# Paged sample attention: keys turned on VectorE in 32x32 blocks instead of on TensorE, scores by 32x32 tiles, and the past bias laid out to match

## What is computed

```python
past_k  = cache_fox_k[page_table].reshape(db, past_len, H_F, D_F)      # db 8, past_len 4096, H_F 8, D_F 64
past_v  = cache_fox_v[page_table].reshape(db, past_len, H_F, D_F)
past_lf = cache_fox_logf[page_table].reshape(db, past_len, H_F)
c_all = cumsum(concat([past_lf, logf], axis=1), axis=1)
s = einsum('bqhd,bkhd->bhqk', q, concat(past_k, fk)) * D_F ** -0.5
s = s + c_all[query] - c_all[key]                                       # the bias; masked where key > query
p = softmax(s, axis=-1)
o = einsum('bhqk,bkhd->bqhd', p, concat(past_v, fv))                    # then @ w_fox_o, times a sigmoid gate
```

## Time and profile before

| | |
|---|---|
| median of 3 runs | 3672.9 us (3669.8 to 3675.2) |
| the profiled execution | 3673.46 us |
| its span | 3671.6 us |
| granted TensorE clock, mean | 0.949 |
| TensorE busy over the span | 3314.7 us (90%) |
| sample bias phase | 1720 to 1768 us |
| sample attention phase | 2091 to 2616 us |

### The profile page before, as it was taken

How to read it: one execution, slowest core, us unless ns; L and a number is a source line. 1 busy time by engine, 2 the same in 40 slices (tenths; PEclk the granted TensorE clock), 3 DMA queues, 4 the chain that set the end, 5 groups by cost and what they waited for, 6 DMA issues and landing times. The chain is left out here.

```text
span 3671.6 us, 56105 instructions
## 1 busy us (share of the span) xinstructions
PE 3314.7 (90%) x21121; PEld 2999.5 (82%) x21121; DVE 888.4 (24%) x1581; ACT 625.5 (17%) x1163; POOL 794.6 (22%) x696
## 2 busy tenths in 40 slices
PE   5999999997988898786799899999796999999996
PEld 5999999996887798554688666666686999999995
DVE  2111111114206211555101022222314111111114
ACT  3000000002101100344000144434203000000003
POOL 0232222323120131022111111111021223233220
PEclk8999999998997899899899999999798999999998
DMA  5111111111110112210211299999311111111111
GB/s 141 35 51 40 42 49 34 49 49 29 29 44 22 41 40 67 91 48 17 52 43 43 60 297 307 300 305 303 121 29 29 34 46 50 33 51 43 37 37 55
DMA packets 328667, 293.12 MB, mean 80 GB/s; under 512 B 33640, under 2 KB 249064, under 8 KB 328048
## 3 DMA queue, kind: packets, MB, share of 16 engines
q1 hardware_dynamic: 317136, 275.93, 24.3%
q0 software_dynamic: 11424, 15.76, 1.6%
HBM read 279.34 MB, written 12.26 MB: 79 GB/s over the span
## 5 line engine op out<-in xcount | busy, mean ns | idle before, releaser
L207 PE MATMUL f_acc<-x_hi,w_hi_last 128*128 128x364 f32 x1056 | 233.5, 329 | 27.5 <-SPq L489 27.5
L165 POOL CAST w_hi_first<-w_raw_first 128x1024 fp32r<-128x1024 f32 (+1 forms) x96 | 82.9, 863 | 738.4 <-issue 301.3
L207 PE MATMUL f_acc<-x_hi,w_hi_first 128*128 128x364 f32 x1056 | 233.5, 329 | 6.9 <-SPq L489 6.9
L207 PE MATMUL f_acc<-x_lo,w_hi_last 128*128 128x364 f32 x1056 | 234.0, 330 | 0.0
L207 PE MATMUL f_acc<-x_hi,w_lo_last 128*128 128x364 f32 x1056 | 234.0, 330 | 0.0
L207 PE MATMUL f_acc<-x_hi,w_lo_first 128*128 128x364 f32 x1056 | 233.9, 330 | 0.0
L207 PE MATMUL f_acc<-x_lo,w_hi_first 128*128 128x364 f32 x1056 | 233.7, 329 | 0.0
L207 PEld LDWEIGHTS f_acc<-x_hi,w_hi_last 128*128 128x128 f32 x1056 | 184.0, 189 | 28.0 <-issue 28.0
L165 POOL CAST w_hi_last<-w_raw_last 128x1024 fp32r<-128x1024 f32 (+2 forms) x92 | 73.5, 799 | 614.2 <-PE f_acc L207 610.2
L596 DVE SCALAR_TENSOR_TENSOR br<-f_acc,br 128x1092 f32 x88 | 114.1, 1296 | 368.8 <-PE f_acc L207 368.8
L207 PEld LDWEIGHTS f_acc<-x_hi,w_hi_first 128*128 128x128 f32 x1056 | 184.0, 189 | 7.1 <-issue 7.1
(11 more groups left out here) (399 smaller groups left out, 6321.8 us busy)
## 6 DMA issues: line engine op xcount, KB each, us to landing
br<-cache_fox_k SPq DMA_DIRECT2D x256, 256.0 KB, 5.6
br<-cache_fox_v SPq DMA_DIRECT2D x256, 256.0 KB, 6.5
w_raw_first<-w_ffn_gate SPq DMA_DIRECT2D x22, 512.0 KB, 3.8
w_raw_first<-w_ffn_up SPq DMA_DIRECT2D x22, 512.0 KB, 3.8
w_raw_last<-w_ffn_gate SPq DMA_DIRECT2D x22, 512.0 KB, 3.8
w_raw_last<-w_ffn_up SPq DMA_DIRECT2D x22, 512.0 KB, 3.8
w_raw_first<-w_ffn_down SPq DMA_DIRECT2D x40, 256.0 KB, 2.9
w_raw_last<-w_ffn_down SPq DMA_DIRECT2D x40, 256.0 KB, 2.8
```

Source lines behind the costliest of these rows:

```text
L165: self.nc.gpsimd.tensor_copy(hi, raw).then_inc(self.high[s], 1)
L207: mm = self.nc.tensor.matmul(out[:, b, 0:width], w[s][:, k, :], x[:, k, b * width:(b + 1) * width], start=(k == 0 and first), stop=(k == k ...
```

## The change

The work and its result stay what they were. Its parts:

1. **Page table.** One contiguous DMA in place of the two with a stride. The pages come in their natural order.
2. **Bias phase.** The sums are made 32 rows at a time, four of them in one PSUM tile by column group (rows 0 to 31, 32 to 63, and so on), and for every fourth page by itself. That makes 64 pairs of matmuls of 32 rows by 128 columns, 128 matmuls in place of 32, written so that the 8 of one column group follow one another. Their operands are first rearranged: 4 copies on ScalarE (`d_own`), 4 on VectorE (`d_behind`). `d_qz` is no longer made here.
3. **Turning the keys.** VectorE turns a quad by 2 instructions of 128x1024 that transpose every 32x32 block in place, into one of 2 tiles `d_kt`. The 16 transposes of a quad on TensorE and the 4 copies on ScalarE are gone. SP waits for `k_turned` once per half of a chunk instead of once per key page.
4. **Scores.** 64 matmuls per quad, with 32 rows of keys' dimensions, 32 rows of queries and 128 columns each: 4 row groups of the array write 4 PSUM banks, 4 column groups are 4 pairs of heads, and 4 matmuls add up in each place. The queries lie in `d_q_rep`, which ScalarE fills by 16 small copies per sequence (and 2 for the new tokens' `d_qz`).
5. **Behind the scores.** All heads' pages have their own column group, so a step has 512 columns for VectorE's minimum and ScalarE's exponentials (before: 256), 4 turns of probabilities (before: 2), 16 products of 128 columns (before: 8 of 256), and `d_acc` of 128 columns (before: 256). The copy to `d_pt` moves from VectorE to ScalarE. `d_stp`, `d_ptp` and `d_ov` have one buffer instead of two, so that `scores(k)` waits for the minimum of step k - 1. `swap`, `comb` and the combining at a sequence's end are gone.
6. **Fillers.** The gate and the `w_fox_o` product take the prompt in 3 blocks of up to 364 columns in place of 2 of 512 and a rest of 64.
7. **Ring.** The bias is loaded into `mem_kt` and `mem_v`, in 128 DMAs of 64 KB where there were 64 of 128 KB.

The core of the diff:

```diff
-                for e in range(2):
-                    half = g.pages[:].rearrange("o (b n e) -> o b n e", b=NSEQ, e=2)[:, :, :, e]
-                    sp.dma_start(half, io["page_table"][:, e * (NPG // 2):(e + 1) * (NPG // 2)].unsqueeze(0),
-                                 allow_slow_non_contiguous=True).then_inc(consts, 16)
+                sp.dma_start(g.pages[:], io["page_table"].rearrange("b n -> (b n)").unsqueeze(0)).then_inc(consts, 16)
...
                 pe.wait_ge(copied, 2)
-                pe.wait_ge(steps, 6)
+                pe.wait_ge(own_ok, QUAD)
+                pe.wait_ge(behind_ok, QUAD)
                 for c in range(2 * NSEQ):
                     if c == NSEQ:
                         pe.wait_ge(read, 1)
                     b, x = divmod(c, 2)
-                    own = lft[:, b, x * HG:(x + 1) * HG, :].rearrange("p g h -> p (g h)")
-                    behind = tot[1][:, b, x * HG + 1:(x + 1) * HG + 1, :].rearrange("p g h -> p (g h)")
-                    nc.tensor.matmul(sums[:, c % NSEQ, :], own, after[:], start=True, stop=False)
-                    mm = nc.tensor.matmul(sums[:, c % NSEQ, :], behind, g.ones[:], start=False, stop=True)
+                    group, pages = slice(ROWS * (c % 4), ROWS * (c % 4 + 1)), slice(x * QUAD, (x + 1) * QUAD)
+                    for n in range(QUAD):
+                        at = by_token[group, c // 4 % 2, n]
+                        nc.tensor.matmul(at, own[:, b, n, pages, :].rearrange("p u h -> p (u h)"), after[:],
+                                         start=True, stop=False, skip_group_check=True)
+                        mm = nc.tensor.matmul(at, behind[:, b, n, pages, :].rearrange("p u h -> p (u h)"), g.ones[:],
+                                              start=False, stop=True, skip_group_check=True)
...
+                for n in range(QUAD):
+                    nc.scalar.copy(own[:, :, n], lft[:, :, n:NPG:QUAD]).then_inc(own_ok, 1)
...
+                for n in range(QUAD):
+                    nc.vector.tensor_copy(behind[:, :, n], tot[1][:, :, n + 1:NPG + 1:QUAD]).then_inc(behind_ok, 1)
...
-                sp.dma_start(swap[:], io["swap"]).then_inc(const, 16)
-                sp.dma_start(comb[:], io["comb"]).then_inc(const, 16)
...
                 with sp.Fori(0, CHUNKS - 1) as c:
                     ahead, now = pages(c + 1), pages(c)
                     for half in range(2):
+                        sp.wait_ge(k_turned, c * 4 + (2 * half + 2))
                         for s in range(half * QUAD, (half + 1) * QUAD):
-                            sp.wait_ge(k_turned, c * CH + (s + 1))
-                            sp.dma_start(k_in[:, s, :], keys[ahead[s]].rearrange("t h d -> t (h d)")).then_inc(k_ok[s], 16)
-                        sp.wait_ge(valued, c * 8 + (4 * half + 4))
+                            load_key(s, ahead[s])
+                        sp.wait_ge(valued, c * 2 + (half + 1))
...
+                    out = stp_pages.rearrange("p n (f t) -> p n f t", f=QUAD)
+                    for s in range(2):
+                        for h in range(2):
+                            for x in range(4):
+                                rows = slice(ROWS * x, ROWS * (x + 1))
+                                for c in range(PAIRS):
+                                    block = 4 * c + 2 * s + h
+                                    q = q_rep[e][rows, block * QW - s * LSEQ:block * QW - s * LSEQ + ROWS]
+                                    mm = nc.tensor.matmul(out[ROWS * c:ROWS * (c + 1), x], q,
+                                                          kt[u % 2][rows, :, block * ROWS:(block + 1) * ROWS],
+                                                          start=(s == 0 and h == 0), stop=(s == 1 and h == 1),
+                                                          skip_group_check=True)
+                    mm.then_inc(scored, 1)
...
+                    for y in range(QUAD if v else 1):
+                        if v:
+                            n = u * QUAD + y
+                            pe.wait_ge(v_ok[n % CH], 16 * (n // CH + 1))
+                        for c in range(PAIRS):
+                            values = v_in[:, n % CH, c * P:(c + 1) * P] if v else g.v_s[0:TS, c * P:(c + 1) * P]
+                            mm = nc.tensor.matmul(ov[ROWS * c:ROWS * (c + 1), :],
+                                                  pt[0:P if v else TS, y, ROWS * c:ROWS * (c + 1)], values,
+                                                  start=(y == 0), stop=(y == QUAD - 1 or not v), skip_group_check=True)
+                    mm.then_inc(valued if v else new_valued, 1)
...
                 for k in range(STEPS_ALL + 4):
-                    u = quad_after(k)
-                    if u is not None:
-                        turn(u, 0)
-                        turn(u, 1)
+                    if k < STEPS_ALL:
+                        scores(k)
                     if 0 < k <= STEPS_ALL:
                         turn_probs(k - 1)
+                    fill(k)
                     if k >= PIECES + 1 and (k - 1) % PIECES == 0:
-                        swap_stats((k - 1) // PIECES - 1)
-                    if k >= PIECES + 2 and (k - 2) % PIECES == 0:
-                        turn_out((k - 2) // PIECES - 1)
-                    fill(k)
-                    if u is not None:
-                        turn(u, 2)
-                        turn(u, 3)
-                    if k < STEPS_ALL:
-                        scores(k)
+                        turn_out((k - 1) // PIECES - 1)
                     if 0 < k <= STEPS_ALL:
                         products(k - 1)
...
+                    nc.scalar.activation(out, least, ACT.Exp, bias=nm[e][:, v:v + 1], scale=-1.0,
                                          accum_out=lp[e][:, v:v + 1]).then_inc(exped, 1)
...
+                    nc.scalar.copy(pt[0:rows, 0:n], ptp[0:rows, 0:n]).then_inc(pt_ok, 1)
...
+                def turn(u):
+                    for s in range(u % 2 * QUAD, (u % 2 + 1) * QUAD):
+                        dve.wait_ge(k_ok[s], 16 * (u // 2 + 1))
+                    if u >= 2:
+                        dve.wait_ge(scored, step_of(u - 2) + 1)
+                    for y in range(2):
+                        nc.vector.transpose(kt[u % 2][:, 2 * y:2 * y + 2, :], k_in[:, u % 2, 2 * y:2 * y + 2, :])\
+                            .then_inc(k_turned, 1)
...
                 for k in range(STEPS_ALL + 4):
-                    if 0 < k <= STEPS_ALL:
-                        place(k - 1)
-                    if k >= PIECES + 1 and (k - 1) % PIECES == 0:
-                        finish((k - 1) // PIECES - 1)
-                    if k >= PIECES + 2 and (k - 2) % PIECES == 0:
-                        output((k - 2) // PIECES - 1)
-                    add_mix(k)
```

More of the change, by code:

```diff
@@ L2146, in phase_sample_bias @@
         after, upto = g.sb(ctx, "d_after", [P, P]), g.sb(ctx, "d_upto", [TS, TS])
-        mask, lfx = g.sb(ctx, "d_mask", [P, NSEQ, TS]), g.sb(ctx, "d_lfx", [TS, 2, 2, 4, LSEQ])
-        out = g.sb(ctx, "d_out", [P, 2 * NSEQ, P])
+        mask, lfx = g.sb(ctx, "d_mask", [P, NSEQ, TS]), g.sb(ctx, "d_lfx", [TS, PAIRS, ROWS])
+        own, behind = (g.sb(ctx, f"d_{x}", [P, NSEQ, QUAD, NPG // QUAD, H_F]) for x in ("own", "behind"))
+        out = g.sb(ctx, "d_out", [P, NSEQ // 2, QUAD * P])
         t = [g.ps(ctx, f"d_t{j}", [P, H_F, P]) for j in range(2)]
-        sums = g.ps(ctx, "d_sums", [P, NSEQ, P])
+        sums = g.ps(ctx, "d_sums", [P, 2, QUAD * P])
         cn = g.ps(ctx, "d_cn", [P, TS])
@@ L2498, in turn_probs @@
                     else:
-                        half, m = divmod(b * (PIECES - 1) + v - 1, QUAD)
-                        for x in range(2):
-                            mm = nc.tensor.transpose(ptp[:, k % 2, x, :], ring[half % 2][:, m, x, :], g.ident[:])
+                        for y in range(QUAD):
+                            mm = nc.tensor.transpose(ptp[:, y, :], probs[:, y, :], g.ident[:])
                     mm.then_inc(pturned, 1)
@@ L2505, in scores @@
                     b, v = divmod(k, PIECES)
[L2506 to L2519 removed]
+                    e, u = b % 2, b * (PIECES - 1) + v - 1
@@ new lines, in scores @@
+                    if k > 0:
+                        pe.wait_ge(topped, k)
+                    if k >= PIECES + 2 and v == 2:
+                        pe.wait_ge(out_ok, b)
+                    if v == 0:
+                        pe.wait_ge(q_ok, 18 * (b + 1))
+                        for c in range(PAIRS):
+                            mm = nc.tensor.matmul(stp[ROWS * c:ROWS * (c + 1), 0, 0:TS], qz[e][:, c, :], g.k_s[:, c, :],
+                                                  start=True, stop=True)
+                        mm.then_inc(scored, 1)
+                        return
@@ L2560, in gate_part @@
+                    nc.tensor.transpose(ot, on[:], g.ident[:]).then_inc(ot_ok, 1)
+                def gate_part(j, x, ks):
+                    if ks[0] == 0 and 4 * j + x > 0:
```

(11 more changed lines are left out.)

407 lines of the change are left out of this document (180 added, 227 removed).

## The result

| | before | after |
|---|---|---|
| median | 3674.1 us (4 runs, 3669.8 to 3675.7) | 3747.6 us (4 runs, 3743.7 to 3756.8) |
| profiled span | 3671.6 us | 3747.4 us |
| ratio | | 1.0206 (95%: 1.0184 to 1.0227) |

The change costs 74 us, twice the 37 that were forecast, and 5.6 us beyond the end of the range. In the two spans the 75.8 us divide as follows, by the starts of SP's first and last issues in each phase: load phase -3.8 us (the bias phase's first issue comes at 1716.88 instead of 1720.66), bias phase +17.3, loop of the sample phase to its last value pages +66, tail and the rest -4.

The account below looks back on a forecast made before the run. It took SP's queue as the bound, with instruction fetches lengthening issues they meet. Terms -2 + 22 - 1 - 6 + 20 + 3 + 1 = +37 on 3673.5 us gave 3710 us; range 3670 to 3742.

Parts of the forecast that it names:

- load phase: Page table loading: one contiguous issue replaces two strided ones of 1.53 us in all; -2 us (0 to -3).
- bias phase: Serial sums before the sample phase: four VectorE copies and 128 records per half instead of 32; +22 us (+7 to +26).
- tail: Last steps after the last page: a little longer in matmuls; +1 us.
- start of the sample phase: Head of SP's queue: one table load of 0.35 us and its twin leave; -1 us.
- SP's register instructions: SP's loop: eight register instructions in front of key issues leave, part returning as a wait; -6 us (0 to -12).
- instruction packets that meet SP's issues: SP's loop: about 60 more instruction fetches, lengthening issues by 0.34 us each on average; +20 us (0 to +63).
- SP's waits in the loop: Sample phase: late value pages' places at sequence ends, with single buffers, make SP wait; +3 us (0 to +20).
- TensorE per step: Sample phase: scores of 0.9 us, a step of 4.2 to 4.8 us against SP's 7.7 per quad; term 0.
- The start of records decides: Rival, scores: TensorE begins at most one record per 62 ns, deciding above 30 ns; +256 us, 3966; 8% with anything worse.
- VectorE, or the single buffers, late: Rival, sample phase: transposes of 2.6 us and waits between engines push a quad past 7.7 us; +20, 3730 us; 8%.
- The overlap in the bias phase: Rival, bias phase: column groups run beside each other, making the phase's term +7; 3695 us; 15%.

Follow-up runs that it names:

- before_numbers_once: The kernel before, with SP's loop written out so that each page number is loaded into a register once instead of twice: 3632.9 us, ratio 0.9884.
- the control: The kernel before, with 4 matmuls of 128 columns on one column group added ahead of each quad's scores, which overwrite them: 3688.3 us, ratio 1.0044.
- VectorE's order: The changed kernel, turning the next quad's keys before this step's minimum: 3748.4 us; together with 32 score matmuls of 256 columns per quad: 3706.1 us.
- bias_by_columns: The changed kernel with the bias phase's 128 matmuls reordered, so the column group changes at each matmul instead of after 8: 3734.6 us, ratio 1.0175.
- before_more_instructions: The kernel before, with 56 matmuls of 4 columns added ahead of each quad's scores, which overwrite them: 3789.5 us, ratio 1.0315.

## Why the prediction was wrong

Right were the bound of the kernel before, which before_numbers_once confirmed, and the sign. Its terms:

| step | forecast | measured |
|---|---|---|
| load phase | -2 | -3.8 |
| bias phase | +22 | +17.3 |
| start of the sample phase | -1 | about 0 |
| SP's register instructions | -6 | -4 (ALU instructions 9.3 to 3.1 us, others 2 us more) |
| instruction packets that meet SP's issues | +20 | +15 (overrun 24.5 to 39.8 us) |
| SP's waits in the loop | +3 | +58 |
| tail | +1 | -3 to -4, with what lies behind it |

Seven terms, six of them within 5 us, read one by one from the traces (they add up to 79, not 76). The +15 stands against 55 more packets in the loop (34 before, 89 after; some 60 were forecast).

**The step that failed is "TensorE per step"**, with its sentence that TensorE has over 2.9 us to spare and its term is 0 up to 3.8 us of scores, and with it the +3 for waits: they came to 58 us more. Two things were wrong in it.

It counted the array's time, and got that too small. It has 4.2 to 4.8 us a step where TensorE is busy 7.1 us a quad, so that 0.6 us of SP's 7.7 were to spare and not 2.9. 128 score records take 1.64 us at the full clock, not 0.9. The pieces of the gate and of the `w_fox_o` product came to 3.1 us a quad, not 2.0 to 2.6. They have 364 columns in place of 512, but there are three of them in place of two and a small rest: 192 records of 364 columns for each kind of gate matmul, where 128 of 512 and 64 of 64 stood, which is as many columns. And 72 steps, not 64, fall on the 64 quads. The clock was granted less besides. The earlier trace rows had the check: 465.64 / 510 x 7.73 = 7.1 us busy a quad before, of which the turns that leave are 1.94. A busy TensorE is not yet late: before_numbers_once ran at 7.07 us a quad with TensorE busy 98%, and the control shows 0.86 us more per quad costing 16 us.

What the step left out is that the records have to be brought. The prediction had the packets, and their number nearly right, but looked at them only as something that SP's issues run into. The engine that consumes them stood in no term, although and the earlier trace rows gave the quotient: one packet per 232 to 250 records, and a quad of the change has some 360 records, where it had 130. Stops of up to 3.6 us followed, 69.6 us in all.

How much of the 58 us is theirs is only in part known. Without the stops the kernel is 29 us faster and SP's waits for keys are 41 us in place of 61; the shorter burst of scores has a share in the 29 that was not taken apart. VectorE's order gives some 13 us more, and about 23 us of waits stay open.

The rivals did no better. "The start of records decides" named the right engine with the wrong price: its point of 30 ns was not reached. "VectorE, or the single buffers, late" has a +20 that is near SP's waits at sequence ends, but for a transposing instruction of 2.6 us, and it took 1.2; 13 us by VectorE's order were shown. The overlap in the bias phase was refused for the right reason: the column group changed too seldom, and bias_by_columns showed what it is worth when it changes each time.

The Trainium skill's page "TensorE: Matmul & The Clock Gate", Part 1, gives some 25 ns as the least from start to start. The 12.9 ns of the 32x32 tiles (128 records in 1.64 us), and 8.5 ns in before_more_instructions (112 records in 0.94 us), are under it; the measurement decides.

## What to carry to other kernels

Count instructions per step as well as columns. Here TensorE's written-out program went by faster than its packets came, with the DMA engines some 90% busy with pages, and it stopped for up to 6 us at a time; "issue" in its waits, ending just behind an instruction packet, is how that looks. Whether it would stop as well with idle DMA engines was not tried. Check a forecast of an engine's time per step against its busy time in the profile before: the parts that stay must add up to it. To find a bound, take work out of the queue that is suspected and see whether it comes back as waits. Small matmuls on different column groups ran side by side when neighbours in the program changed the group: 64 of them took 3.8 us, and 11.4 when 8 in a row shared a group.

## What was not expected

- 224 more records per quad, of 4 columns each, cost the kernel before 100 us beyond what as long a piece of plain matmuls costs, though the packets that carry them are about 1% of the DMA engines' time.
- Taking half of the score instructions away was enough to remove the stops. MATMUL records in 440 us, and "issue" in TensorE's waits: 4050, none; 6040, 3 us; 8042, 54 us; 9018, 70 us. Nothing between 6040 and 8042 was measured, and the kernels differ in more than this number.
- A block transpose of 128x1024 float32 on VectorE took 1222 ns, the price of an operation with two inputs and not of a copy (690 ns).
